# Three float32r passes with split operands for the second output projection of a two-layer hybrid decoder

## The chip, the cores and the metric

The kernel runs on one core of one Trainium2 chip, in float32. The metric is device time of one launch in microseconds (us), the median of the timed runs; less is better. TensorE (PE in the rows) multiplies, PEld is its weight load, VectorE is DVE, ScalarE is ACT, GpSimd is POOL, SyncE is SP; a q behind a name is that engine's queue.

## The reference

Two decoder layers over 512 tokens of width 1024. Each is mixer, layer norm, mixture of experts, layer norm and a gated injection. Layer 1's mixer is sparse latent attention, whose heads are joined and then mapped by one output projection:

```python
def mixer_c(x, w_in, q_norm, kv_norm, w_uq, w_uk, w_uv, w_out):
    ...
    o = lax.map(block, jnp.arange(T // Q_BLOCK))
    o = o.transpose(1, 0, 2, 3).reshape(B, T, C_HEADS * C_HEAD_DIM)
    return o @ w_out
...
def reference(...):
    for i in range(DEPTH):
        ...
        x = layer_norm(ALPHA * x + h.astype(x.dtype), ln1_g[i], ln1_b[i])
        m = hierarchical_moe(x, moe_w_group[i], moe_b_group[i], moe_w_expert[i], moe_b_expert[i],
                             moe_w_gu[i], moe_w_down[i])
        x = layer_norm(ALPHA * x + m, ln2_g[i], ln2_b[i])
        x = x + jax.nn.sigmoid(x @ ple_w_gate[i]) * (p[i] @ ple_w_proj[i])
```

`o` and `w_out` are 512x1024 and 1024x1024. `hierarchical_moe` chooses two of 32 experts for a token; an expert's weights are 1024x1024 for gate and up and 512x1024 for down, 6,144 KB together.

## The kernel before

The program is a row of blocks, each with its own instruction lists for the engines, written out by hand with semaphores; a block begins once all engines have left the one before. For layer 1 the blocks are `latents` (projections into latent space and the choice of keys), `attention`, `out_projection` (with the first layer norm, the turned copy XT of the tokens and the router's logits), `route` (which token goes to which slot of which expert) and `experts` (all 32 experts, then the second norm and the injection).

**Attention.** Tokens form four tiles of 128 (T = 4). A unit is one tile and one head; 64 units run in the order tile 3, 2, 1, 0, with 512, 384, 256 and 128 keys. All engines go through the same counter i and each works on a unit some steps behind it: TensorE scores unit i, turns unit i-6 and multiplies unit i-8 with the values; VectorE (L1893) adds the mask; ScalarE (L1919) takes the exponential; VectorE inverts the sum of unit i-2 (L1899); GpSimd (L1935) multiplies the row by it, except every fourth unit, which VectorE multiplies at step i+3 (L1904); ScalarE copies three of four turned units out of PSUM (L1838), VectorE every fourth (L1883). `finish` copies the results of half a tile's heads out of PSUM bank 6 or 7 into MC, a view of `slim[1]`: ScalarE the first half at step 0 of the next tile (L1838), VectorE the second half at step 8 (L1834), both once more behind the last unit.

**Output projection.** `out_projection` computes four tiles in two halves of 512 columns, each half in a PSUM bank over KD = 8 products (L639), `sums.full` counting the halves. VectorE adds each half to the tokens (L662), takes statistics (L190) and normalises (L198, L202); TensorE turns the tile back (L162) and computes router logits (L633) from the copy that ScalarE makes (L169). The weights w_out lie in `wide[0]`, loaded during `latents`.

**Memory and loads.** `wide[0]`, `wide[1]` (32 KB a partition) and `slim[0]`, `slim[1]` (16 KB) are two areas for experts, `pair[0]` = (`wide[1]`, `slim[0]`) and `pair[1]` = (`wide[0]`, `slim[1]`). SP issues all weight transfers in order. `load_gu` (L429) loads gate and up as two transfers of 2,048 KB, `load_dn` (L433) down as one, `load_third_gu` (L438) a third expert's gate and up into w3 and w4, `load_third_dn` (L442) its down matrix into XT. Expert 0 goes into `pair[0]` and, in `out_projection`, is loaded by `load_first` while the products run; expert 1 goes into `pair[1]` behind the last half (`then_load`, which waits for `sums.full`, 8th count, and stands behind the stores of the normalised tokens, L694, and the loads of the next norm's vectors, L211 and L212). In `experts` SP issues the next load of an area when TensorE has read the half that lay there. The rows of tokens for an expert are gathered by GpSimd (L871), turned (L883), multiplied (L898 gate and up, L912 down) and scattered (L877).

The first layer's input projection (L405) already works in float32r: ScalarE rounds an operand to float32r (L305, L314), VectorE subtracts that from the operand (L336, L343), and each float32 product becomes three of float32r: high times high, high times low, low times high.

## Time and profile before

| what | value |
|---|---|
| median of 3 runs (lowest, highest) | 1667.98 us (1664.65, 1668.8) |
| the profiled execution | 1662.05 us |
| its span, first to last instruction | 1660.2 us |
| TensorE busy | 1435.3 us, 86% |
| VectorE, ScalarE, GpSimd busy | 406.8, 305.6, 188.8 us |
| moved by DMA | 482.55 MB, mean 291 GB/s |
| layer 1: attention | 930.8 to 1013.9 us of the span |
| layer 1: output projection and first norm | 1014.3 to 1085 |
| layer 1: router, experts, injection | 1085 to the end |

Times in the rows are microseconds from the span's start. Where a row names what ended an engine's idle time, that is inferred from semaphores. An engine that is busy most of a stretch need not be what bounds it; what ends the waits says that.

### The profile page before, as it was taken

Reading aid. Unit: us, or ns where it says so; the run is one execution under the profiler, and the core shown is the slowest. Engines: PE = TensorE matmul, PEld = TensorE weight load, DVE = VectorE, ACT = ScalarE, POOL = GpSimd, SP = SyncE. Lnnn points to the kernel's source line nnn. Section 1 sums busy time; section 2 is a strip of 40 time slices with the busy share of each in tenths; the row PEclk is TensorE's granted clock in tenths of the full one; section 3 lists DMA queues with packets and bytes.
Section 4 is the critical chain, followed back from the end, with each engine's and each line's share of the span. In section 5 each row is a group of like instructions: output and inputs, shape, how many; then the busy total and the mean of one; then the engine's idle time right before and its main releaser. Section 6 shows DMA issues by size and latency. Waiting matters only on the chain. (4 is left out here: it accounts for less than half of the span.)

```text
span 1660.2 us, 16843 instructions
## 1 busy us (share of the span) xinstructions
PE 1435.3 (86%) x6032; PEld 656.7 (40%) x6032; DVE 406.8 (25%) x1016; ACT 305.6 (18%) x622; POOL 188.8 (11%) x317
## 2 busy tenths in 40 slices
PE   6998978998888789879999989959988788889887
PEld 5885443332223233224444454533322223333333
DVE  3424341000000011044068353340000000011072
ACT  3212011111011011012234563011111011101121
POOL 0000001221111111100000221011111111111100
PEclk9999978999999999999999999969999999999999
DMA  7106357999999999994200004279999999999840
GB/s 283 51 26 266 139 201 314 396 427 430 429 428 429 428 429 428 425 376 165 108 1 1 1 2 187 122 304 385 429 429 428 431 429 428 429 428 426 362 189 38
DMA packets 78305, 482.55 MB, mean 291 GB/s; under 512 B 18400, under 2 KB 20452, under 8 KB 45480
## 3 DMA queue, kind: packets, MB, share of 16 engines
q1 hardware_dynamic: 65800, 463.76, 67.2%
q0 software_dynamic: 10240, 16.82, 2.7%
q10 hardware_dynamic: 2208, 1.20, 0.2%
q8 instruction: 37, 0.61, 0.1%
q14 instruction: 20, 0.16, 0.0%
HBM read 474.91 MB, written 23.59 MB: 300 GB/s over the span
## 5 line engine op out<-in xcount | busy, mean ns | idle before, releaser
L898 PE MATMUL PS<-wide,w 128*64 128x512 f32 x1984 | 447.3, 600 | 47.6 <-ACT w L917 29.0
L912 PE MATMUL PS<-slim,w 128*64 128x512 f32 x992 | 256.2, 663 | 77.4 <-issue 76.1
L898 PEld LDWEIGHTS PS<-wide,w 128*64 128x64 f32 x1984 | 136.6, 137 | 326.5 <-issue 259.5
L912 PEld LDWEIGHTS PS<-slim,w 128*64 128x64 f32 x992 | 85.0, 150 | 242.8 <-issue 240.6
L924 DVE TENSOR_TENSOR w<-w,PS 128x256 f32<-128x256 f32 x64 | 26.9, 421 | 530.9 <-ACT w L921 530.9
L1164 PE MATMUL PS<-wide,XT 128*128 128x512 f32 x256 | 116.5, 612 | 2.3 <-ACT XT L169 2.3
L921 ACT ACTIVATE w<-PS 128x256 f32<-128x256 f32 x64 | 24.6, 384 | 498.9 <-PE PS L898 498.9
L927 DVE COPY w<-PS 128x256 f32<-128x256 f32 x64 | 27.2, 425 | 300.0 <-PE PS L905 300.0
L1477 ACT ACTIVATE w<-PS,w 128x512 f32<-128x512 f32 x62 | 42.6, 688 | 315.2 <-PE PS L912 315.2
L1344 POOL COPY w<-w 128x1 uint32 (+1 forms) x62 | 11.3, 182 | 656.7 <-ACT w L1477 656.7
L1164 PEld LDWEIGHTS PS<-wide,XT 128*128 128x128 f32 x256 | 49.3, 196 | 62.8 <-issue 59.6
L871 POOL DMA_INDIRECT w<-x_rows,w x64 | 67.2, 1050 | 55.0 <-POOL w L1337 53.7
L877 POOL DMA_INDIRECT y_rows<-w x62 | 63.6, 1027 | 54.8 <-POOL w L1344 54.8
L639 PE MATMUL PS<-wide,slim 128*128 128x512 f32 x128 | 56.0, 594 | 1.1 <-PEq L1840 1.1
L883 PE MATMUL PS<-ident,w 128*128 128x128 f32 x256 | 42.8, 291 | 8.3 <-DMA w<-x_rows,w 8.2
L169 ACT ACTIVATE XT<-PS 128x512 f32<-128x512 f32 x40 | 21.7, 594 | 149.6 <-PE PS L162 149.6
L917 ACT ACTIVATE w<-PS 128x512 f32<-128x512 f32 x64 | 38.2, 597 | 44.5 <-PE PS L883 42.8
L405 PE MATMUL PS<-x_high,w_high 128*128 128x512 f32 x96 | 38.2, 398 | 8.1 <-DVE w_low L343 8.1
L905 PEld LDWEIGHTS PS<-ident,w 128*128 128x128 f32 x128 | 20.1, 206 | 56.7 <-issue 53.0
L1935 POOL TENSOR_SCALAR w<-w 128x512 f32<-128x512 f32 (+3 forms) x48 | 26.6, 555 | 128.2 <-DVE w L1899 127.7
L883 PEld LDWEIGHTS PS<-ident,w 128*128 128x128 f32 x256 | 36.8, 211 | 9.4 <-DMA w<-x_rows,w 9.4
L1919 ACT ACTIVATE w<-w 128x512 f32<-128x512 f32 (+3 forms) x64 | 35.6, 556 | 23.9 <-DVE w L1893 23.7
(225 smaller groups left out, 1494.5 us busy)
## 6 DMA issues: line engine op xcount, KB each, us to landing
wide<-in_moe_w_gu SPq DMA_DIRECT2D x124, 2048.0 KB, 25.4
slim<-in_moe_w_down SPq DMA_DIRECT2D x62, 2048.0 KB, 25.4
w<-in_moe_w_gu SPq DMA_DIRECT2D x4, 2048.0 KB, 18.7
wide<-in_ple_w_gate SPq DMA_DIRECT2D x4, 2048.0 KB, 13.8
w<-in_ab_w_in SPq DMA_DIRECT2D x2, 2048.0 KB, 14.0
w_in<-in_ab_w_in SPq DMA_DIRECT2D x2, 2048.0 KB, 7.5
x_rows<-X SPq DMA_DIRECT2D x8, 512.0 KB, 2.8
XT<-in_moe_w_down SPq DMA_DIRECT2D x2, 2048.0 KB, 20.8
```

Of the source, the lines that this page charges most:

```text
L405: m = pe.matmul(PS[:, j % 8, :], lhsT, rhs, start=(k == 0 and r == 0), stop=(k == KD - 1 and r == 2))
L639: m = pe.matmul(PS[:, 2 * t + c, :], mixed[:, k, t * P:(t + 1) * P], w_halves[c][:, k, :], start=(k == 0), stop=(k == KD - 1))
L871: pool.indirect_dma_start(out=xg[q], out_offset=None, in_=x_half, in_offset=bass.IndirectOffsetOnAxis(ap=index, axis=0), bounds_check=2 * ...
L877: pool.indirect_dma_start(out=y_rows, out_offset=bass.IndirectOffsetOnAxis(ap=index, axis=0), in_=ys[q], in_offset=None, bounds_check=4 * ...
L883: m = pe.transpose(PS[:, q, c * P:(c + 1) * P], xg[q].rearrange("p (f c) -> p c f", c=4)[:, c, :], ident[:, :])
L898: m = pe.matmul(PS[u * SLOTS:(u + 1) * SLOTS, 2 + q, :], xeT[q][:, k, :], gu[k].rearrange("p (a u c) -> p a u c", a=2, u=2)[:, :, u, :], s ...
L912: m = pe.matmul(PS[u * SLOTS:(u + 1) * SLOTS, 6 + q, :], gT[:, k, :], dn[k][:, u * NB:(u + 1) * NB], start=(k == 0), stop=(k == FF // P - 1))
L917: return act.activation(xeT[q].rearrange("p (u c) s -> p c u s", u=2), PS[:, q, :].rearrange("p (c u s) -> p c u s", c=4, u=2), ACT.Copy)
L927: return dve.tensor_copy(gT.rearrange("p (u c) s -> p c u s", u=2), PS[:, 4 + q, 0:2 * P].rearrange("p (c u s) -> p c u s", c=2, u=2))
L1164: m = pe.matmul(PS[:, self.gate_bank(u), :], XT[:, k, t * P:(t + 1) * P], WG[:, k, c * NB:(c + 1) * NB], start=(k == 0), stop=(k == KD - 1))
L1477: act.activation(ys[q], PS[:, 6 + q, :], ACT.Copy, scale=R["gate_of"][:, bass.ds(expert(q, i), 1)]).then_inc(s_y[q], 1)
L1919: act.activation(g, g, ACT.Exp, bias=nmax[:, i:i + 1], scale=-1.0, accum_out=rsum[:, i:i + 1]).then_inc(s_p, 1)
```

## The change

1. `out_projection` takes its products from a function. For layer 0 they are as before. For layer 1 each float32 product becomes three of float32r, 192 instead of 64.
2. The operands are split during attention. `finish` becomes two steps: ScalarE copies a half bank into `mixed_high` (float32r, in `slim[1]`), then VectorE subtracts it from the bank into `mixed_low` (in the first half of `wide[1]`). ScalarE does so for both halves (steps 0 and 8), VectorE at steps 2 and 10. For the weights ScalarE copies a piece of 128x512 into `w_out_high` (second half of `wide[1]`, and `slim[0]`) at every fourth step, and GpSimd subtracts it from the raw weights into `w_out_low`, in place in `wide[0]`: 16 pieces.
3. Since `wide[1]` and `slim[0]` now hold split operands until the last product, expert 0's three transfers move from `load_first` to `then_load`, ahead of expert 1's.

```diff
-        def out_projection(l, mixed, w_halves, w_sems, load_first, then_load):
+        def out_projection(l, products, w_sems, load_first, then_load):
...
-                            for k in range(KD):
-                                m = pe.matmul(PS[:, 2 * t + c, :], mixed[:, k, t * P:(t + 1) * P],
-                                              w_halves[c][:, k, :], start=(k == 0), stop=(k == KD - 1))
+                            pairs = products(t, c)
+                            for r, (lhsT, rhs) in enumerate(pairs):
+                                m = pe.matmul(PS[:, 2 * t + c, :], lhsT, rhs, start=(r == 0),
+                                              stop=(r == len(pairs) - 1))
...
+        MCH = three(again("mixed_high", "slim1", 0, 4096)[:, :], SEQ)
+        MCL = three(again("mixed_low", "wide1", 0, 4096)[:, :], SEQ)
+        WO = three(wide[0][:, :], D)
+        WOL = three(again("w_out_low", "wide0", 0, 8192)[:, :], D)
+        WOH = [three(again("w_out_high0", "wide1", 4096, 4096)[:, :], D), three(again("w_out_high1", "slim0", 0, 4096)[:, :], D)]
...
+            def finish_high(act, half, nth):
+
+                high, low, ps = mixed_of(half, nth)
+                act.wait_ge(s_pv, AH // 2 * nth + 4 * half + 4)
+                act.activation(high, ps, ACT.Copy).then_inc(s_mh, 1)
+
+            def finish_low(dve, half, nth):
+
+                high, low, ps = mixed_of(half, nth)
+                dve.wait_ge(s_mh, 2 * nth + half + 1)
+                dve.tensor_tensor(low, ps, high, ALU.subtract).then_inc(s_o[half], 1)
...
-                        if i % AH == 8 and i >= AH:
-                            finish(dve, dve.tensor_copy, 1, i // AH - 1)
-                    finish(dve, dve.tensor_copy, 1, T - 1)
+                        if i % AH == 2 and AH <= i < N:
+                            finish_low(dve, 0, i // AH - 1)
+                        if i % AH == 10 and AH <= i < N:
+                            finish_low(dve, 1, i // AH - 1)
+                    finish_low(dve, 0, T - 1)
+                    finish_low(dve, 1, T - 1)
...
+                        if i % 4 == 2 and i < N:
+                            raw, high, low = out_pieces(i // 4)
+                            if i < 4:
+                                act.wait_ge(s_cwout, 16)
+                            act.activation(high, raw, ACT.Copy).then_inc(s_wh, 1)
+                    finish_high(act, 0, T - 1)
+                    finish_high(act, 1, T - 1)
...
+                        if i % 4 == 3:
+                            raw, high, low = out_pieces(i // 4)
+                            pool.wait_ge(s_wh, i // 4 + 1)
+                            pool.tensor_tensor(low, raw, high, ALU.subtract).then_inc(s_wl, 1)
...
         def before_out(l):
             def load_first(sp):
-                if l == 1:
-                    load_gu(sp, 1, 0, 0)
-                    load_dn(sp, 1, 0, 0)
                 load_third_gu(sp, l)
...
         def after_out(l):
             def then_load(sp, sums):
                 sums.wait_full(sp, 7)
+                if l == 1:
+                    load_gu(sp, 1, 0, 0)
+                    load_dn(sp, 1, 0, 0)
                 load_gu(sp, l, 1, 1)
                 load_dn(sp, l, 1, 1)
...
+            high = [WOH[k // 4][:, k % 4, cs] for k in range(KD)]
+            return [pair for k in range(KD) for pair in ((MCH[:, k, ts], high[k]), (MCH[:, k, ts], WOL[:, k, cs]),
+                                                         (MCL[:, k, ts], high[k]))]
```

What stands in a row on the engines is shown at two places. First, the whole of GpSimd's list in attention (buffer numbers are left out in names; w is one of w1 to w4). Before:

```order
L1928 UNCONDITIONAL_BRANCH
L1935 ISA
L1935 TENSOR_SCALAR w<-w 128x512 x12
L1935 TENSOR_SCALAR w<-w 128x384 x12
L1935 TENSOR_SCALAR w<-w 128x256 x12
L1935 TENSOR_SCALAR w<-w 128x128 x12
```

After, its beginning, in tile 3:

```order
L1973 ISA
L1973 TENSOR_SCALAR w<-w 128x512 x3
L1977 TENSOR_TENSOR w_out_low<-wide,w_out_high_1105 128x512
L1973 TENSOR_SCALAR w<-w 128x512 x3
L1977 TENSOR_TENSOR w_out_low<-wide,w_out_high_1105 128x512
```

A subtraction stands behind every third multiplication, through all tiles.

ScalarE at the change from tile 3 to tile 2. Before (L1919 the exponential, L1838 with `w<-PS` the copy of a turned unit, with `slim<-PS` the `finish` copy):

```order
L1919 ACTIVATE w<-w 128x512
L1919 ACTIVATE w<-w 128x384
L1838 ACTIVATE w<-PS 128x512
L1838 ACTIVATE slim<-PS 128x4x128
L1919 ACTIVATE w<-w 128x384
```

After:

```order
L1865 ACTIVATE w<-PS 128x512
L1962 ACTIVATE w_out_high_1105<-wide 128x512
L1949 ACTIVATE w<-w 128x512
L1949 ACTIVATE w<-w 128x384
L1865 ACTIVATE w<-PS 128x512
L1856 ACTIVATE mixed_high<-PS 128x4x128
L1949 ACTIVATE w<-w 128x384
```

A piece of the weights now stands ahead of the last exponential of a group of four units.

Second, SP's list in the output projection of layer 1, and what follows it. Before:

```order
L682 DMA w<-in_moe_b_expert 128x32
L429 DMA wide<-in_moe_w_gu 128x4096 x2
L433 DMA slim<-in_moe_w_down 128x2x2048
L438 DMA w<-in_moe_w_gu 128x4096 x2
...
L694 DMA x_rows<-X 128x1024 x4
L211 DMA ln_g<-in_ln_g 128x1024
L212 DMA ln_b<-in_ln_b 128x1024
L429 DMA wide<-in_moe_w_gu 128x4096 x2
L433 DMA slim<-in_moe_w_down 128x2x2048
L624 UNCONDITIONAL_BRANCH
```

After:

```order
L690 DMA w<-in_moe_b_expert 128x32
L445 DMA w<-in_moe_w_gu 128x4096 x2
...
L702 DMA x_rows<-X 128x1024 x4
L218 DMA ln_g<-in_ln_g 128x1024
L219 DMA ln_b<-in_ln_b 128x1024
L436 DMA wide<-in_moe_w_gu 128x4096 x2
L440 DMA slim<-in_moe_w_down 128x2x2048
L436 DMA wide<-in_moe_w_gu 128x4096 x2
L440 DMA slim<-in_moe_w_down 128x2x2048
L631 UNCONDITIONAL_BRANCH
```

Three transfers of 2,048 KB moved from the start of the block to its end, in front of three others and of the branch that ends the block.

## Rows read from the trace of the kernel before

**Rows 1.** The page: span, GB/s in 40 equal slices, expert weight loads.
```profile
span 1660.2 us, 16843 instructions
...
GB/s 283 51 26 266 139 201 314 396 427 430 429 428 429 428 429 428 425 376 165 108 1 1 1 2 187 122 304 385 429 429 428 431 429 428 429 428 426 362 189 38
...
wide<-in_moe_w_gu SPq DMA_DIRECT2D x124, 2048.0 KB, 25.4
```

**Rows 2.** The chain that ended last, within layer 1's experts: start, us, what.
```profile
1258.72 26.64 DMA wide<-in_moe_w_gu
...
1285.41 3.68 PE PS L898 x16
```

**Rows 3.** Stretches: length, busy per engine (count), clock, DMA share, GB/s.
```profile
1104.00:1120.00 16.00, 10.53 (x42) 4.03 (x42) 5.43 (x21) 2.86 (x4) 2.82 (x5) 0.76 0.51 187
1120.00:1150.00 30.00, 28.59 (x136) 10.31 (x138) 1.69 (x4) 3.34 (x6) 4.90 (x8) 1.00 0.93 372
...
1240.00:1540.00 300.00, 252.46 (x1082) 90.34 (x1079) 23.40 (x49) 32.09 (x58) 46.61 (x76) 0.95 1.01 429
```

**Rows 4.** Timeline, both projections: start, us, engine, line, operation, idle before.
```profile
1059.18 7.03 PE L639 MATMUL PS<-wide,slim 128*128 128x512 f32 x16
1066.06 1.87 PE L633 MATMUL PS<-w,XT 128*128 128x36 f32 x16
...
86.29 0.39 PE L405 MATMUL PS<-w_high,x_high 128*128 128x512 f32 x1
...
129.58 0.39 PE L405 MATMUL PS<-w_high,x_low 128*128 128x512 f32 x1
...
1074.91 0.69 DVE L662 SCALAR_TENSOR_TENSOR X<-X,PS 128x512 f32<-128x512 f32 x1 [7.24 <-PE PS L639]
...
1078.00 1.28 DVE L202 SCALAR_TENSOR_TENSOR X<-X,rstd,ln_b 128x1024 f32<-128x1024 f32 x1
```

**Rows 5.** Attention and the first split: groups, a stretch, and timeline rows.
```profile
L314 ACT ACTIVATE w_high<-w_in 128x1024 fp32r<-128x1024 f32 x4 | 4.0, 1049 | 5.2 <-DMA w_in<-in_ab_w_in 5.2
...
L336 DVE TENSOR_TENSOR x_low<-PS,x_high 128x512 fp32r<-128x512 f32 x8 | 4.9, 683 | 8.6 <-ACT x_high L305 8.6
...
996.80:1013.90 17.10, 13.86 (x119) 8.45 (x118) 9.00 (x61) 11.83 (x51) 4.95 (x13) 1.00 0.01 1
...
1000.69 0.40 ACT L1919 ACTIVATE w<-w 128x128 f32<-128x128 f32 x1 [0.45 <-DVE w L1893]
...
946.06 0.69 POOL L1935 TENSOR_SCALAR w<-w 128x512 f32<-128x512 f32 x1 [1.34 <-DVE w L1899]
950.31 0.85 POOL L1935 TENSOR_SCALAR w<-w 128x512 f32<-128x512 f32 x1 [3.56 <-DVE w L1899]
...
1000.83 0.37 POOL L1935 TENSOR_SCALAR w<-w 128x128 f32<-128x128 f32 x1 [0.69 <-DVE w L1899]
1003.12 0.84 POOL L1935 TENSOR_SCALAR w<-w 128x128 f32<-128x128 f32 x2 [1.92 <-DVE w L1899]
```

**Rows 6.** Timeline: the last two `finish` copies of attention.
```profile
1012.62 0.60 ACT L1838 ACTIVATE slim<-PS 128x512 f32<-128x512 f32 x1
...
1013.35 0.69 DVE L1834 COPY slim<-PS 128x512 f32<-128x512 f32 x1 [1.40 <-PE PS L1871]
```

**Rows 7.** Timeline of SP's queue behind the output projection.
```profile
1082.08 0.91 SPq L429 DMA_DIRECT2D wide<-in_moe_w_gu  x2
1083.03 0.96 SPq L433 DMA_DIRECT2D slim<-in_moe_w_down  x1
...
1114.10 10.03 SPq L429 DMA_DIRECT2D wide<-in_moe_w_gu  x3
```

**Rows 8.** The chain: the first gather, and one within the plateau.
```profile
1101.08 6.07 DMA w<-x_rows,w
...
1195.69 9.03 DMA w<-x_rows,w
```

More of the change, by code:

```diff
@@ L54, in build, with again @@
     with ctx:
+        home = {}
         def sb(name, shape, dt=F32):
+            home[name] = -(-nc.sbuf_base // 32) * 32
             return ctx.enter_context(nc.sbuf_tensor(name, shape, dt))
+        def again(name, of, first, n):
+            return nc.alloc_sbuf_tensor_at(name, [P, n], F32R, offset=home[of] + 4 * first)
         def lasting(name):
@@ L1810, in build, with out_pieces @@
         rden = w2[:, 2176:2240]
-        MC = three(slim[1][:, :], SEQ)
+        MCH = three(again("mixed_high", "slim1", 0, 4096)[:, :], SEQ)
[3 more added lines that the diff above has]
+        WOH = [three(again("w_out_high0", "wide1", 4096, 4096)[:, :], D), three(again("w_out_high1", "slim0", 0, 4096)[:, :], D)]
+        def out_pieces(p):
+            k, cs = p // 2, slice((p % 2) * NB, (p % 2 + 1) * NB)
+            return WO[:, k, cs], WOH[k // 4][:, k % 4, cs], WOL[:, k, cs]
         def attention():
@@ L1824, in attention, with mixed_of @@
             s_ptc = [sem(f"{n}_ptc_{e}") for e in ("act", "dve")]
-            s_o = [sem(f"{n}_o_{e}") for e in ("act", "dve")]
+            s_o = [sem(f"{n}_o_{half}") for half in range(2)]
+            s_mh, s_wh, s_wl = sem(f"{n}_mixed_high"), sem(f"{n}_w_high"), sem(f"{n}_w_low")
             def so_far(owner, j):
                 return owner[:j + 1].count(owner[j])
-            def finish(eng, copy, half, nth):
+            def mixed_of(half, nth):
                 t = ORDER[nth]
-                eng.wait_ge(s_pv, AH // 2 * nth + 4 * half + 4)
-                copy(MC[:, 4 * half:4 * half + 4, t * P:(t + 1) * P], three(PS[:, 6 + half, :], P))\
-                    .then_inc(s_o[half], 1)
+                return [m[:, 4 * half:4 * half + 4, t * P:(t + 1) * P] for m in (MCH, MCL)] + [three(PS[:, 6 + half, :], P)]
+            def finish_high(act, half, nth):
[6 more added lines that the diff above has]
+                dve.tensor_tensor(low, ps, high, ALU.subtract).then_inc(s_o[half], 1)
             def plain(act):
@@ L1923, in _ @@
                             copy_turned(act, plain(act), j)
-                        if i % AH == 0 and i >= AH and i < N:
-                            finish(act, plain(act), 0, i // AH - 1)
-                    finish(act, plain(act), 0, T - 1)
+                        if i % AH == 0 and AH <= i < N:
+                            finish_high(act, 0, i // AH - 1)
+                        if i % AH == 8 and AH <= i < N:
+                            finish_high(act, 1, i // AH - 1)
+                        if i % 4 == 2 and i < N:
[5 more added lines that the diff above has]
+                    finish_high(act, 1, T - 1)
                 @block.gpsimd
@@ L1935, in _ @@
                             pool.tensor_scalar(g, g, rden[:, i:i + 1], 1.0, ALU.mult, ALU.mult).then_inc(s_n[0], 1)
+                        if i % 4 == 3:
+                            raw, high, low = out_pieces(i // 4)
+                            pool.wait_ge(s_wh, i // 4 + 1)
+                            pool.tensor_tensor(low, raw, high, ALU.subtract).then_inc(s_wl, 1)
+                    pool.wait_ge(s_wl, N // 4)
             Stages.end()
@@ L1971, in store_tiles, with first_products, second_products @@
             sp.wait_ge(s_out, 16 * T)
-        out_projection(0, MT, w_out0, s_wout, before_out(0), after_out(0))
+        def first_products(t, c):
+            return [(MT[:, k, t * P:(t + 1) * P], w_out0[c][:, k, :]) for k in range(KD)]
+        def second_products(t, c):
+            ts, cs = slice(t * P, (t + 1) * P), slice(c * NB, (c + 1) * NB)
+            high = [WOH[k // 4][:, k % 4, cs] for k in range(KD)]
+            return [pair for k in range(KD) for pair in ((MCH[:, k, ts], high[k]), (MCH[:, k, ts], WOL[:, k, cs]),
+                                                         (MCL[:, k, ts], high[k]))]
+        out_projection(0, first_products, s_wout, before_out(0), after_out(0))
         layer_end(0, next_layer_loads, lambda sp, s_done: None, True)
@@ L1976, in build @@
         attention()
-        WO = three(wide[0][:, :], D)
-        out_projection(1, MC, [WO[:, :, 0:NB], WO[:, :, NB:D]], [s_cwout], before_out(1), after_out(1))
+        out_projection(1, second_products, [s_cwout], before_out(1), after_out(1))
         layer_end(1, lambda sp, norm: None, store_tiles, False)
```

## The prediction

> **What bounds the kernel now.** I read the page first. Its GB/s line has two plateaus near 429, one for each layer's mixture-of-experts stage [rows 1]; the second covers about 460 of the span's 1660.2 us. The chain that ended last shows what holds such a plateau: between two runs of L898, the gate/up products, lies a transfer of a weight half that takes 26.64 us from issue to landing, and L898 starts again as it lands [rows 2]. So there the weight stream, not TensorE, sets the pace. The stretches by time say when that stream is full: its DMA share is 1.01 at 429 GB/s from 1240 to 1540, but only 0.51 between 1104 and 1120 and 0.93 from there to 1150 [rows 3]. Before the plateau the engines set the pace. The output projection of layer 1 (L639) kept TensorE busy, while VectorE waited 7.24 us for its last half tile [rows 4]; the layer norm, router and gather that follow wait for it.
>
> So there are two currencies. Time saved ahead of 1082 moves the start of the weight stream earlier, us for us; bytes moved behind 1082 lengthen the stream, unless they fall into the hole at 1104.
>
> **Step 1, the products: 11.4 us less.** Sixteen recorded passes of L639 are eight float32 products, one half tile: they started at 1059.18 and the next group (L633) at 1066.06 [rows 4], so 6.88 us, 0.859 us a product, and 55.0 us for 64. The new loop issues 192 float32r products of the same shape and operand order. The first projection (L405) already has such: 192 of them from 86.29 to 129.58, hence (129.58 - 86.29) / 191 = 0.2266 us each [rows 4], and 192 cost 43.5 us. They come in the same groups of 24 for one bank, and one half tile costs 5.4 us, so a tile 10.9. VectorE's work on the second half of a tile ran from 1074.91 to 1078.00 + 1.28 [rows 4], 4.4 us, and on the first half it has two more passes of 0.69: about 6 of 10.9, so it stays ahead, and the tail behind the last product is as before. 55.0 - 43.5 = 11.5; I take 11.4 for the change of pitch at group edges. The bounds: the same 192 products at 0.2266, and nothing saved if they went at 0.286 us.
>
> The Trainium skill (FP8 and Floating Point Precision, TensorE Precision Notes) says that full float32 takes four passes through the array. Three passes would then cost three quarters, the step would save 13.7 us, and the total would be 2.3 us lower. The rows give 3 x 0.2266 / 0.859 = 0.79, and the rows decide.
>
> **Step 2, the weight split during attention: 0.3 us more.** ScalarE gets 16 copies of 128x512 and 4 more `finish` copies, GpSimd 16 subtractions, VectorE 4 more `finish` passes. All of it sits in loops that are waited for, so each needs cover.
>
> ScalarE: a copy of 128x512 took 0.60 us [rows 6], and a float32r copy of 128x1024 1.049 [rows 5]. I take 0.6 for a piece; twenty make 12 us. ScalarE is busy 11.83 of 17.10 us even in the last, tightest tile [rows 5]. A copy stands behind unit 4k+2, and the next two-unit step begins with ScalarE waiting 0.45 us for VectorE [rows 5]. So 0.6 us is mostly absorbed within two steps. Ends: 0 and 12 us; I take 0.3, near the bottom, since ScalarE is idle for 5 of those 17 us.
>
> GpSimd: the trace has no two-input operation on it. One input of 128x512 took 0.69 and one of 128x128 0.37 us [rows 5], so 0.83 ns a column over 0.26. Two inputs cost between 0.69 and, with the column price doubled, 1.11. The subtraction stands behind the third of each three multiplications. There GpSimd waits: from 946.75 to 950.31 (3.56 us) in the widest tile, 1.92 us in the narrowest [rows 5]. Either value is hidden.
>
> VectorE: the half-bank copies at step 8 go; two subtractions come at steps 2 and 10, 0.683 us each by the like operation of the first projection [rows 5]. VectorE waits in front of most steps for a score, and these steps are not those in which TensorE waits for its turned copy. Nothing.
>
> **Step 3, the end of attention: 0.7 us more.** Before, ScalarE (1012.62) and VectorE (1013.35) emptied the last two banks independently [rows 6]. Now the last bank goes through ScalarE (0.6) and then VectorE (0.68). So VectorE's operation starts one ScalarE copy and a hand-over later.
>
> **Step 4, the preload: 4.3 us more.** The SP queue issued the first two transfers behind the projection at 1082.08 and the third at 1083.03 [rows 7]: expert 1's weights. Now expert 0's three transfers of 2,048 KB go ahead of them: 6.29 MB. At 0.429 MB/us [rows 3] they are 14.7 us of stream. What do they displace? In the hole the stream lacks (1.01 - 0.51) x 16 = 8.0 us of full share, and from 1120 to 1150 (1.01 - 0.93) x 30 = 2.4 [rows 3]. Together 10.4: 14.7 - 10.4 = 4.3 us that the stream ends later against its own start. By bytes instead of share the hole is 9.0 + 4.0 = 13.0, the loss 1.7; that is the low end. The high end is 14.7, if none of the hole were filled. It is filled as long as the first refill, issued at 1114.10 after half of expert 0's products [rows 7], comes before the longer backlog ends. The 8.0 us missing ahead of that refill put the old backlog's end near 1106, so the new one ends near 1121. Expert 0's own weights are first in the queue: 6.29 MB behind 1082 are in by about 1098, and its first product comes later than the gather's landing at 1107 [rows 8].
>
> A new delay lies here: the first gather now meets a full stream. It took 6.07 us when the stream was running dry, and 9.03 in the plateau [rows 8]. So expert 0 starts up to 3 us later, and the refill comes near 1117, still before 1121. It costs nothing more.
>
> **The sum.** -11.4 + 0.3 + 0.7 + 4.3 = -6.1 us. The profiled execution took 1662.05 us (span 1660.2), which becomes 1655.9. It lies 5.9 under the median of 1667.98, on which I predict: 1661.9 us, 0.37% less. A measurement of this kernel can tell about 0.3%, 5.0 us, from no change.
>
> **Rivals.**
> A, **the stream runs dry after all.** For: SP issues three more transfers before the barrier that opens the router, and the gather waits 3 us longer. A refill after 1121 leaves a hole, us for us. With 3 us from the gather and up to 4 from SP it is just reached, and then the 2.4 us missing behind 1120 stay too: some 3 us are lost, 1664.9, no change. Against: SP needed 1.9 us for its three [rows 7].
>
> B, **the preload is free.** If TensorE rather than the stream bounded the stage, only -10.4 stays: 1657.6. For: near the plateau's end the chain runs over TensorE for long. Against: the share stays at 1.01 to 1540 [rows 3].
>
> C, **attention becomes slower than the products gain.** The mechanism is GpSimd's subtraction: multiplications of the next group queue behind it, and TensorE's turns need them. Between 3.56 and 1.92 us of cover I interpolate 3.0 and 2.5 for the middle tiles. At 3.0 us a subtraction, four groups in each of the last two tiles lose 0.5 and 1.1: 6.4 us, the whole gain. At 3.5 us: 4 x (0.5 + 1.0 + 1.6) = 12.4, and 1674.3 us. Against: it takes nearly three times the doubled price of step 2. A row that speaks for friction is the multiplication at 950.31: 0.85 us instead of 0.69, beside VectorE's division [rows 5]. The Trainium skill (SBUF — State Buffer, Who interferes with whom) says that GpSimd and VectorE's fast mode take a shared port by turns, each for a whole instruction. By that rule a subtraction that outlasts its cover would hold up VectorE's division too, which would make the rival dearer; inside the cover it changes nothing.
>
> D, **the float32r products do not keep their pitch** with operands split elsewhere and a router in between: at 0.25 us 48.0 instead of 43.5, and 1666.4, no change. Against: 192 in a row kept it [rows 4].
>
> **Chances.** Forecast 0.55; A 0.20; B 0.07; C 0.10; D 0.08. The forecast lies 1.1 us beyond the edge of what can be told, so about a quarter of it counts as no change, and a third of A as faster: faster 0.41 + 0.06 + 0.07 = 0.54, slower 0.10, the same 0.36. The range takes in step 4's low end and B below, A and D above: 1656.5 to 1668.0.
>
> **What would show it.** Step 1: 192 products at 0.227 us, the last bank full about 10.4 us earlier against the span's start. Step 2: attention still about 83 us, GpSimd's subtractions near 1.1 us, and its waits shorter by that. Step 3: a ScalarE and then a VectorE row at the end. Step 4: a DMA share near 1 from the first load on without the hole, expert 0 starting 2 to 3 us later behind the router than before, and the plateau's end about 6 us earlier. I am wrong if subtractions exceed 2 us, if the share drops below 0.9 once the stream has begun, or if the last weight half lands less than 4 us earlier.

## The result, and the profile after

| | median (runs) | profiled | span |
|---|---|---|---|
| before | 1666.76 (1662.70 to 1672.85, 6) | 1662.05 | 1660.2 |
| after | 1657.32 (1655.17 to 1659.17, 6) | 1657.87 | 1656.0 |

The ratio is 0.9949 (95%: 0.9934 to 0.9963), so 8.5 us faster by the ratio (6.2 to 11.0). The forecast was 1661.9, in a range from 1656.5: the measured median lies in the range, 0.8 us above its low end.

The page of after, span and GB/s in 40 slices, for [rows 1]:

```profile
span 1656.0 us, 17015 instructions
...
GB/s 284 51 26 267 138 217 297 387 428 429 428 429 430 428 429 428 420 384 186 108 1 0 1 1 115 74 423 404 429 428 428 430 430 428 428 430 427 372 174 38
```

Stretches of after (length, then busy us and count per engine, granted clock, DMA share, GB/s). The first is attention; the others answer [rows 3]:

```profile
932.52:1017.68 85.16, 72.55 (x608) 44.37 (x608) 50.30 (x232) 67.07 (x201) 46.28 (x64) 1.00 0.01 1
...
1080.00:1094.00 14.00, 6.27 (x40) 5.95 (x40) 8.44 (x48) 1.45 (x9) 1.10 (x4) 0.50 1.01 429
...
1104.00:1110.00 6.00, 6.00 (x20) 1.81 (x22) 0.00 (x0) 1.19 (x1) 1.07 (x1) 0.65 1.02 424
1110.00:1120.00 10.00, 8.37 (x42) 3.07 (x40) 0.84 (x2) 0.98 (x2) 0.00 (x0) 1.00 1.02 436
...
1130.00:1140.00 10.00, 9.31 (x48) 3.41 (x44) 0.84 (x2) 1.67 (x3) 1.23 (x2) 1.00 0.89 358
...
1240.00:1530.00 290.00, 243.21 (x1054) 87.77 (x1056) 22.55 (x47) 31.30 (x56) 46.59 (x76) 0.96 1.01 428
```

The hole at 1104 is gone, as predicted; one of 0.89 is left at 1130 to 1140, just under the 0.9 that the prediction had named as a sign of being wrong. Attention takes 85.2 us. Before, the same stretch (from the exponential's table load to the first load of `out_projection`) took 83.5:

```profile
930.79:1014.32 83.53, 71.75 (x600) 43.66 (x598) 48.53 (x229) 66.00 (x198) 46.18 (x64) 1.00 0.01 1
```

The timeline of the projection in after (start, us, engine, line), for [rows 4]; L647 is the product, L670 VectorE's addition, L209 the end of the norm:

```profile
1054.78 0.39 PE L647 MATMUL PS<-w_out_high,mixed_high 128*128 128x512 f32 x1
1055.01 0.40 PE L647 MATMUL PS<-w_out_low,mixed_high 128*128 128x512 f32 x1
...
1067.03 0.69 DVE L670 SCALAR_TENSOR_TENSOR X<-X,PS 128x512 f32<-128x512 f32 x1 [5.86 <-PE PS L647]
...
1070.11 1.29 DVE L209 SCALAR_TENSOR_TENSOR X<-X,rstd,ln_b 128x1024 f32<-128x1024 f32 x1
```

From the projection's start to the last full bank it is 1067.03 - 1017.68 = 49.35 us; before, with the 1074.91 of [rows 4], 1074.91 - 1014.32 = 60.59. That is 11.2 us less. SP's queue behind it in after, for [rows 7], and below it one row of before that stands in the same place as 1072.27:

```profile
1072.27 0.78 SPq L219 DMA_DIRECT2D ln_b<-in_ln_b  x1
1073.09 1.33 SPq L436 DMA_DIRECT2D wide<-in_moe_w_gu  x2
...
1109.79 13.45 SPq L436 DMA_DIRECT2D wide<-in_moe_w_gu  x4
```
```profile
1080.15 1.89 SPq L212 DMA_DIRECT2D ln_b<-in_ln_b  x1
```

Two times of these rows are used for every kernel below: S, the first expert load behind the projection (1073.09; before 1082.08), and R, the first refill (1109.79; before 1114.10). What after's first gather and expert 0's products took, by the chain and the timeline, for [rows 8]:

```profile
1093.79 8.30 DMA w<-x_rows,w
```
```profile
1103.95 9.16 PE L906 MATMUL PS<-wide,w 128*64 128x512 f32 x32 [0.69 <-ACT w L925]
...
1115.72 7.09 PE L906 MATMUL PS<-wide,w 128*64 128x512 f32 x32 [0.69 <-ACT w L925]
```

**Where the time went**, from attention's start to the span's end, by these rows: attention +1.63; projection to S, 1073.09 - 1017.68 = 55.41 against 67.76, -12.35; S to the end, 582.9 (1656.0 - 1073.09) against 578.1 (1660.2 - 1082.08), +4.8. Sum -5.9 (723.5 against 729.4), where -6.1 was forecast. On the span's own clock the last weight half landed only 4.3 us earlier (1539.96 + 24.97 against 1543.87 + 25.39, by the chains), where about 6 was forecast and less than 4 was to be a sign of being wrong. For attention itself began 1.7 us later in this profile, though nothing ahead of it was changed: TensorE's granted clock was 0.84 from 890 to 900, where in the kernel before it was 1.00. A second profile of after (`after_again`) began at 930.41 and took 723.3 from there.

### The profile page after: what moved, and what is told of

It is laid out like the page before. It is cut to its first block and busy times, and to the rows that moved or that the text cites. A ratio compares the mean times of both kernels' runs of the same rounds, so it can differ in the third digit from the quotient of the medians.

```text
span 1656.0 us, 17015 instructions
## 1 busy us (share of the span) xinstructions
PE 1425.3 (86%) x6096; PEld 669.3 (40%) x6096; DVE 409.6 (25%) x1020; ACT 314.9 (19%) x642; POOL 208.4 (13%) x333
## 5 line engine op out<-in xcount | busy, mean ns | idle before, releaser
L1352 POOL COPY w<-w 128x1 uint32 (+1 forms) x62 | 11.2, 181 | 660.8 <-ACT w L1485 660.8
L891 PE MATMUL PS<-ident,w 128*128 128x128 f32 x256 | 42.8, 291 | 11.5 <-DMA w<-x_rows,w 11.1
L1920 DVE CUSTOM_DVE_ANT_0 w<-PS,w 128x512 f32<-128x512 f32 (+2 forms) x48 | 26.3, 551 | 51.8 <-PE PS L1877 51.8
## 6 DMA issues: line engine op xcount, KB each, us to landing
wide<-in_ple_w_gate SPq DMA_DIRECT2D x4, 2048.0 KB, 13.7
w<-in_ab_w_in SPq DMA_DIRECT2D x2, 2048.0 KB, 13.6
```

The costliest lines, as they stand in the source:

```text
L891: m = pe.transpose(PS[:, q, c * P:(c + 1) * P], xg[q].rearrange("p (f c) -> p c f", c=4)[:, c, :], ident[:, :])
```

## The experiments

A table of all profiled kernels comes first, since most of the argument stands on it. `lost` is the time that the stream did not move bytes in the 80 us behind S: 80 x (1 - GB/s / 429), the GB/s from the stretch S to S+80. Three of these stretches (before, after, warm_again):

```profile
1082.08:1162.08 80.00, 61.48 (x291) 28.94 (x293) 19.00 (x89) 10.61 (x23) 13.79 (x22) 0.81 0.87 349
```
```profile
1073.09:1153.09 80.00, 58.38 (x272) 27.93 (x272) 18.61 (x89) 11.68 (x25) 12.07 (x20) 0.78 0.99 408
```
```profile
1069.42:1149.42 80.00, 69.98 (x321) 32.44 (x322) 18.63 (x89) 11.18 (x25) 13.83 (x22) 0.94 1.01 418
```

| kernel | S | R | lost | end | end-R | end-S-lost |
|---|---|---|---|---|---|---|
| before | 1082.1 | 1114.1 | 14.9 | 1660.2 | 546.1 | 563.2 + 14.7 |
| before_look | 1082.9 | 1116.5 | 18.1 | 1663.9 | 547.4 | 562.9 + 14.7 |
| preload_only | 1081.2 | 1117.2 | 3.4 | 1664.1 | 546.9 | 579.6 |
| after | 1073.1 | 1109.8 | 3.9 | 1656.0 | 546.2 | 579.0 |
| after_again | 1071.0 | 1107.6 | 3.9 | 1653.7 | 546.2 | 578.8 |
| two_passes | 1058.2 | 1094.3 | 4.5 | 1641.2 | 547.0 | 578.5 |
| early_loads | 1065.9 | 1111.8 | 12.3 | 1658.2 | 546.4 | 580.0 |
| half_early | 1064.4 | 1109.9 | 13.6 | 1659.7 | 549.8 | 581.7 |
| late_expert1 | 1072.0 | 1105.6 | 8.2 | 1661.2 | 555.6 | 581.0 |
| pool_twice | 1077.6 | 1114.6 | 6.0 | 1664.1 | 549.5 | 580.6 |
| act_twice | 1077.9 | 1114.7 | 4.1 | 1661.6 | 546.9 | 579.6 |
| warm_fill | 1075.2 | 1106.6 | 2.1 | 1656.5 | 549.9 | 579.2 |
| warm_again | 1069.4 | 1102.6 | 2.1 | 1651.4 | 548.8 | 579.9 |
| warm_early | 1062.5 | 1106.1 | 10.1 | 1652.1 | 546.0 | 579.5 |

In the two kernels with the old preload, 14.7 us of stream (expert 0) lie ahead of S and are added. So the last column is 577.6 to 581.7 in all fourteen: **the end is the stream's start, plus its bytes, plus what it loses at its beginning**, to within 4 us. That is the currency of the prediction's step 4. The balance closes no better than that, so it can't decide about an effect of 1 or 2 us. And where the stream has lost more than some 2 us, R goes with the end: end-R is 546.0 to 547.4 in nine of the eleven kernels other than warm_fill, warm_again and late_expert1. The other two, half_early and pool_twice, lie near 550. In both expert 1's first products ran for a part at half clock (8.78 instead of 7.09 us), but they did in before_look too, at 547.4; so what the 3 us are is open.

**after_again and preload_only.** The changed kernel once more, and before with expert 0's three loads moved behind the projection and nothing else:

```
-                if l == 1:
-                    load_gu(sp, 1, 0, 0)
-                    load_dn(sp, 1, 0, 0)      # in load_first, beside the products
...
+                if l == 1:
+                    load_gu(sp, 1, 0, 0)
+                    load_dn(sp, 1, 0, 0)      # in then_load, ahead of expert 1's
```

> The changed kernel once more. The first profiles read -6.1 us from the start of attention to the end (932.52 to 1656.0 against 930.79 to 1660.2), while the medians read -9.4 and the ratio -8.5 us. Theory (the sum of the four steps, -6.1): with more runs the ratio comes near 0.9963, say 0.9955 to 0.9970. Rival (there is another gain that the profile of that execution missed): it stays at 0.9949 or below, and the profile then shows more than 6.1 us between the same two points.

> The kernel before with expert 0's three loads moved behind the last half tile, nothing else. Theory (the added 6.29 MB fall mostly into the hole of the weight stream): 4.3 us slower, 1.7 to 5. Rival 1 (the stage is not bound by the stream, the preload is free): 0. Rival 2 (nothing of the hole is filled): 14.7 us slower. In the profile the DMA share between the first of these loads and the first refill should be near 1.01 where before it was 0.51, and the first gather should land 2 to 3 us later after its issue.

Measured: after_again 1656.63 (1655.87 to 1658.37, 6 runs), 0.9953 (0.9935 to 0.9971), between its two expectations and with an interval that holds both. preload_only 1666.65 (12 runs), 1.0015 (1.0 to 1.003): 0 to 5 us slower, middle 2.5. Its profile gives 733.1 us from attention's start to the end. That is 3.7 more than before's first profile (729.4), but only 0.5 more than before's second (before_look below, 732.6). By the table the stream got 14.7 us longer and lost 11.5 less than in the first, net 3.2, and 14.7 less than in the second, net 0. So what the preload costs depends on how wide the hole is in the execution that it is compared with. The forecast of 4.3 is in the runs' interval, in its upper half.

**two_passes** leaves out the product of the high piece of the activations and the low piece of the weight, one of the three that make a float32 product. It is there for the price, not for use:

```
-  return [pair for k in range(KD) for pair in ((MCH[:, k, ts], high[k]), (MCH[:, k, ts], WOL[:, k, cs]),
-                                               (MCL[:, k, ts], high[k]))]
+  return [pair for k in range(KD) for pair in ((MCH[:, k, ts], high[k]), (MCL[:, k, ts], high[k]))]
```

> The changed kernel without the product high x low: 128 instead of 192 float32r products, one of three passes left out; all splitting as before. Theory (time ahead of the weight stream goes through us for us, since both the stream's start and the router move): 64 x 0.2266 = 14.5 us faster than the changed kernel. Rival (something else is next in the projection, VectorE's norm of about 5.9 us a tile against 7.3 of products): 10 us or less.

Measured: 1643.59, ratio 0.9876 (0.9852 to 0.9899), 13.0 below after_again. The projection's last bank was full 34.87 us behind its start, 14.5 earlier than the 49.35 of after and just 64 x 0.2266. Of that 13.1 arrived at S: the issue of `ln_b` ahead of the loads took 2.12 us here, as in before (1.89), and 0.78 in after. Why it takes either is open. From S on nothing changed. So time saved in the products arrives at the end, less what the issue of one small load took back.

**early_loads, late_expert1, half_early, warm_early** move the loads against the router. early_loads issues all six loads of experts 0 and 1 once the last bank is full and the last tile's store to `x_rows` from ScalarE's queue; half_early only expert 0's two wide loads, ahead of that store on SP:

```
 for t in range(T):
+    if l == 1 and t == T - 1:
+        sums.wait_full(sp, 7)
+        load_gu(sp, 1, 0, 0)
     sp.wait_ge(norm.done, t + 1)
     sp.dma_start(x_rows...)
```

late_expert1 instead holds expert 1's three loads back to the start of `experts`. warm_early is half_early with the extra matmuls of warm_fill (below).

> The changed kernel with the six loads of experts 0 and 1 issued as soon as the last half tile is done, ahead of the last store of tokens (which goes through ScalarE's queue instead) and of the norm's vectors: the stream starts some 5 us earlier, near 1067 instead of 1072.5, the router does not. Theory (in the changed kernel the first refill, at 1109.8, meets a stream that has just about run out, so the router's path and the stream bound it together): 1 to 2 us faster than the changed kernel, and the hole ahead of the refill comes back, 3 to 5 us wide. Rival (the stream alone bounds the stage): 5 us faster.

> The changed kernel with expert 1's three loads of layer 1 issued when its experts' stage begins (about 1103) instead of right behind expert 0's: the gather of expert 0's rows then runs with fewer transfers beside it. If only the order of time at which the first refill may start mattered (it would be some 2 us earlier with a gather of 6 us), this would be 2 us faster than the changed kernel, ratio 0.994. If the stream also bounds: the 14.7 us of expert 1 stand in front of the refill, which can move its bytes from about 1118 instead of 1110; some 2 us of that come back in the stretch 1130 to 1150, where the stream has room: 5 to 7 us slower than the changed kernel, ratio 0.998 to 1.0.

> The changed kernel with expert 0's two wide loads of layer 1 issued as soon as the projection's last product is done, ahead of the last tile's store to x_rows (about 1067 instead of 1073); the other loads stay where they are. So the stream of weights starts some 5 us earlier, and the router should not start later, since it waits for the last logits until 1078. Theory (two bounds: the end comes no earlier than the first refill plus 546 us and no earlier than the stream's start plus some 581 us; in the changed kernel the first is the later one by 1.7): the refill stays, so 0 to 1 us slower or faster than the changed kernel, ratio 0.9945 to 0.9955. Rival (the stream's start alone sets the end): 5 us faster, ratio 0.992.

> Both edits together: the extra matmuls at TensorE's idle places (the refill 3.6 us earlier in warm_fill) and expert 0's two wide loads ahead of the last store (the stream 5 us earlier). Theory of two bounds: each edit alone runs into the other bound, both together move both, the refill by 3.6 us and the stream by 5: 3 to 4 us faster than the changed kernel in layer 1, 2 us faster than warm_again, ratio 0.990. Rival 1 (stream's start alone): as half_early, 5 us faster than the changed kernel even without the fillers. Rival 2 (the last store, now behind 4 MB of weights, holds the router back): no faster than warm_again.

Measured: early_loads 1660.62, 0.9975 (0.9963 to 0.9987); late_expert1 1661.18, 0.9980 (0.9969 to 0.9991); half_early 1660.15, 0.9969 (0.9959 to 0.9980); warm_early 1654.84, 0.9941 (0.9928 to 0.9954). None of the first three gains on after, and three expectations of mine fell: early_loads was to be 1 to 2 us faster and is 4 slower, half_early was to be level and is 3 slower, and warm_early was to be 2 us faster than warm_again and is 1.3 slower by the medians, as its rival 2 had it. late_expert1 came out near its second branch (5 to 7 slower), at 4 to 4.5. SP's queue in half_early shows the reason:

```profile
1064.43 0.81 SPq L436 DMA_DIRECT2D wide<-in_moe_w_gu  x2
1068.84 0.33 SPq L705 DMA_DIRECT2D x_rows<-X  x1
...
1079.36 0.38 SPq L449 DMA_DIRECT2D XT<-in_moe_w_down  x1
```

The stream starts 49.3 us behind the projection's start instead of 55.4. But the last store of tokens, 0.5 MB, now goes out behind 4 MB of weights. It landed 10.1 us after its issue, in after 2.9. The block ends only when it has landed, and the next block's first load on SP (L449) comes 149.4 us after attention's start instead of 146.0. It is not the place in SP's queue alone that does it: in early_loads the same store was issued from ScalarE's queue, took 9.8 us, and L449 came 150.8 us after attention's start. The refill follows, the stream runs dry ahead of it (13.6 us lost instead of 3.9), and the early start is given back with interest. Expert 1's products also ran for a part at half clock (8.78 instead of 7.09 us):

```profile
1103.23 9.96 PE L909 MATMUL PS<-wide,w 128*64 128x512 f32 x32 [0.69 <-ACT w L928]
...
1115.81 8.78 PE L909 MATMUL PS<-wide,w 128*64 128x512 f32 x32 [0.69 <-ACT w L928]
```

late_expert1 is the other half: R comes 33.7 us behind S instead of 36.7, since the gather meets less, and it is of no use: the stream stood still ahead of expert 1's loads (8.2 lost), and expert 1's bytes stand in front of the refill's. So neither end alone can be pulled. Whether both together would gain no run shows: warm_early was meant for it, but its early loads hold the store back too (L449 at 149.5 us, R at 178.1 behind attention's start, against 173.8 in warm_again), so its router was not early.

**warm_fill, warm_again.** In after TensorE's granted clock is 0.50 from 1072 to 1104 (its row 1104 to 1110 above: 0.65), a stretch in which it is little busy: norm, router and gather. These kernels give it something to do: float32 matmuls of the identity by 384 columns of X, into a PSUM bank that nobody reads, 19 more in each layer.

```
+        def filler(pe, n, bank):
+            for _ in range(n):
+                pe.matmul(PS[:, bank, P:NB], ident[:, :], X[:, 0, 0:NB - P], start=True, stop=True)
...
+                    filler(pe, 1, 1)     # ahead of logits(T - 2), and of logits(T - 1)
+                    filler(pe, 4, 7)     # start of route
+                    filler(pe, 3, 7)     # behind the rank sums
+                    filler(pe, 10, 6)    # behind the gates' sums in experts
```

> The changed kernel with extra float32 matmuls of the identity by 384 columns of X into a bank of PSUM that nobody reads, at TensorE's idle places of both layers: one each before the last two tiles' logits, 4 at the router's start, 3 after the rank sums, 10 after the gates' sums. The profile of the changed kernel has the granted clock at 1.2 GHz from 1071 to 1107. Theory (the end follows the first refill at a constant 546 us): the turn of the last tile (1.97 to 1.09 us), its logits (3.63 to 1.8), the slots' sum (3.67 to 1.9) and expert 0's first products (9.19 to 7.1) shorten by 6.5 us together in layer 1, the first refill comes 4 to 6.5 us earlier and the end with it; layer 0 gives 0 to 6 more: 4 to 12 us faster than the changed kernel, ratio 0.988 to 0.993. Rival 1 (the stream of weights sets the end by its own start): nothing moves, ratio 0.995. Rival 2 (the clock does not rise for these matmuls, or they get in the way of the real ones): 0 to 5 us slower than the changed kernel, and the windows of the router still show 0.50.

> warm_fill once more, for a second profile (the first fell on the slowest of its five runs, 1658.4 against 1651.2 to 1653.6, with a stretch of half clock in the projection) and to stand beside warm_early. Theory of two bounds: layer 1 gives 1.7 us at most over the changed kernel, since the stream's start bounds it from there, and layer 0 the rest; median 1651 to 1654, ratio 0.992. If layer 1 gives more than 2 us from attention's start to the end (723.4 us in both profiles of the changed kernel), the second bound is wrong.

Measured: 1651.55 (1651.24 to 1658.40, 5 runs), 0.9921 (0.9907 to 0.9935), and 1653.52 (1651.09 to 1655.98, 6 runs), 0.9933 (0.9921 to 0.9946). **This is the fastest version with all three products**: 12 to 13 us under before and 3 to 6 us under after by the medians; the intervals, each against before, touch that of after in warm_fill and overlap it in warm_again. Stretches and rows of warm_again:

```profile
1068.00:1074.00 6.00, 3.54 (x27) 2.84 (x25) 0.00 (x1) 1.17 (x3) 0.00 (x0) 0.95 0.92 265
1074.00:1084.00 10.00, 7.92 (x37) 4.60 (x38) 9.31 (x56) 2.65 (x10) 1.44 (x2) 0.86 1.01 422
1084.00:1094.00 10.00, 9.19 (x35) 6.42 (x35) 5.73 (x26) 0.00 (x0) 3.79 (x6) 0.66 1.02 433
1094.00:1104.00 10.00, 9.31 (x41) 4.25 (x41) 0.20 (x1) 1.88 (x2) 1.25 (x2) 1.00 0.99 419
```
```profile
1082.99 2.00 PE L763 MATMUL PS<-w 128*128 128x64 f32 x16 [0.47 <-DVE w L846]
...
1098.80 7.09 PE L915 MATMUL PS<-wide,w 128*64 128x512 f32 x32 [0.69 <-ACT w L934]
```

The clock stays at 2.4 GHz for most of it (0.95, 0.86, 0.66, 1.00), the slots' sum takes 2.00 instead of 3.67 us and expert 0's products 7.09 instead of 9.16. R comes 173.8 us behind attention's start, 3.5 earlier than in after. But the end comes only 0.8 earlier from there (722.6 against 723.4), in warm_fill not at all. So warm_fill's theory, that the end follows the refill at 546 us, failed in layer 1, though its total came out: the last 1.8 us of the stream's hole are closed, and then the stream's start is the bound, as the table's last column says. The rest of the gain came ahead of attention: it began at 928.81, and the layer 0 experts' stage ended (first load of `y_rows`) at 717.47 instead of 718.65 and 720.55. In the profile of warm_fill the projection itself lost 1.6 us, the clock being 0.74 from 1020 to 1025; it was the slowest of its five runs.

**pool_twice and act_twice** do GpSimd's subtraction, or ScalarE's copy, twice per piece of the weight, the second time into a spare buffer:

```
                             pool.tensor_tensor(w_out_low..., raw, high, ALU.subtract)
+                            pool.tensor_tensor(spare, raw, high, ALU.subtract)
...
+                            act.activation(spare, raw, ACT.Copy)
                             act.activation(w_out_high..., raw, ACT.Copy)
```

> The changed kernel with GpSimd's subtraction for the low piece of the weight done twice per tile, the second into a spare buffer that nobody reads. One subtraction took 1.27 us in the profile of the changed kernel, so two take 2.55. Theory (GpSimd's covers hold, as in the prediction's step 2): the gaps of GpSimd in attention shrink from 3.6 to 1.9 us towards the last tiles, so only the last one or two tiles are late: 1 to 4 us slower than the changed kernel, ratio to the kernel before 0.9955 to 0.9975. Rival (C, GpSimd is the bound, or VectorE is held up beside each subtraction): 16 times about 0.8 to 1.3 us, 12 to 20 us slower than the changed kernel, ratio 1.002 to 1.007.

> The changed kernel with ScalarE's copy for the high piece of the weight done twice per tile, the second into a spare buffer that nobody reads: 16 more copies of 0.62 us, 9.9 us of ScalarE. Theory (step 2: ScalarE waits for VectorE some 16 us during attention, and a copy falls into such a wait): 1 to 3 us slower than the changed kernel, ratio 0.9955 to 0.997. Rival (ScalarE sets attention's pace): all 9.9 us come on top, ratio 1.001.

Measured: pool_twice 1663.96, 0.9987 (0.9973 to 1.0000); act_twice 1663.03, 0.9994 (0.9982 to 1.0006): 6 and 7 us slower than the changed kernel by the ratios, between theory and rival. Attention took 88.3 and 89.3 us instead of 85.2: 3.1 and 4.1, which is the theory for GpSimd and a little above it for ScalarE. The rest is a second price that neither expectation had. Stretches of pool_twice across the end of attention:

```profile
1010.00:1020.00 10.00, 7.20 (x38) 3.73 (x39) 4.85 (x21) 5.72 (x22) 6.71 (x9) 0.57 0.01 2
1020.00:1025.00 5.00, 5.00 (x13) 3.84 (x13) 0.00 (x0) 1.13 (x2) 0.00 (x0) 0.50 0.51 63
```

TensorE's clock falls to 1.2 GHz between 1010 and 1015 in both kernels, and the projection begins in that state. From 1005 to 1010 TensorE was busy 3.48 us in pool_twice and 3.83 in act_twice, in after 4.28; that this tipped it is likely, not shown. From its start to S the projection took 57.9 and 57.3 us instead of 55.4. So 16 subtractions and copies fit where they are, with little to spare. The same trace shows how GpSimd holds up VectorE. A row of 128x128 that VectorE multiplies by the inverted sum (the division) took 0.27 us in the kernel before, and as long as the subtraction beside one:

```profile
1011.86 1.27 POOL L1984 TENSOR_TENSOR w_out_low<-wide,w_out_high 128x512 fp32r<-128x512 f32 x1
1011.92 1.30 DVE L1935 TENSOR_SCALAR w<-w 128x128 f32<-128x128 f32 x1
```

The Trainium skill (SBUF — State Buffer, Who interferes with whom) calls this an exclusive lock of a shared port pair; these two rows agree.

**before_look**, the kernel before once more:

> The kernel before once more, for a second profile: whether the first one's 83.5 us from attention's start to the projection's, its refill (end minus 546 us), and its bytes not moved in the first 90 us of the stream (16 us) are what it does each time. If so, 83.4 to 83.7, 546 to 547 and 15 to 17; span 1660 to 1666.

Measured: 1665.8, span 1663.9; attention to projection 83.55, as in the first profile. But 732.6 us from attention's start to the end, 3.2 more than there, and 18.1 us lost instead of 14.9. The first expected value came out (83.4 to 83.7), the second is just missed (end-R 547.4), the third clearly:

```profile
1109.82 9.98 PE L898 MATMUL PS<-wide,w 128*64 128x512 f32 x32 [0.69 <-ACT w L917]
...
1122.42 8.78 PE L898 MATMUL PS<-wide,w 128*64 128x512 f32 x32 [0.69 <-ACT w L917]
```

In the first profile these were 8.41 and 7.09. More of the products ran at half clock (granted 0.83 from 1114 to 1129 here), the refill came 1.9 us later behind attention's start, and the stream, dry at that time, passed it on. So the profile that the prediction rests on was a lucky one. Against this second profile the changed kernel gained 9.1 us from attention's start to the end (723.5 against 732.6): attention +1.6, projection to S -12.6, S to the end +1.9.

## Why the prediction was right, and where it was not

**Direction and mechanism hold**; the sum was -6.1 and the profiles' own difference from attention's start is -5.9. Term by term:

- **Step 1, -11.4: right.** 11.2 to the last bank, pitch 0.227 to 0.23 (the rows 1054.78 and 1055.01), and two_passes confirms the price of a product. Another 1.1 us came from the shorter issue of `ln_b`, which no step had. Rival D is refuted. The Trainium skill (FP8 and Floating Point Precision, TensorE Precision Notes) says four passes for full float32, by which three would have saved 13.7 us; the trace does not agree, with 11.2 us and three products at 0.79 of one.
- **Step 2, +0.3: too small.** From attention's start to the first `finish` behind the last unit it is 1015.36 - 932.52 = 82.8 against 81.8 with the 1012.62 of [rows 6], so +1.0. One price in it was wrong outright, GpSimd's subtraction. I put it between 0.69 and 1.11; the groups of after read

```profile
L1977 POOL TENSOR_TENSOR w_out_low<-wide,w_out_high 128x512 fp32r<-128x512 f32 x16 | 20.4, 1275 | 0.0
...
L1962 ACT ACTIVATE w_out_high<-wide 128x512 fp32r<-128x512 f32 x16 | 9.9, 617 | 0.0
```

  so 1.275 us, beyond my upper end: the second input cost more than doubling the column price allows. The Trainium skill (GPSIMD Engine Reference, 3.1 Elementwise — side-by-side cycle accounting) states about 2.6 cycles an element for a `tensor_tensor` with two inputs. At the page's 1.2 GHz that is an estimate of 1.11 us for 512 columns, and 1.37 with the fixed 0.26 us of my own fit: an upper end that would have held 1.275. I had not used it. The cover held in the wide tile, where the next multiplication comes 2.3 us after the subtraction is done:

```profile
948.82 1.28 POOL L1977 TENSOR_TENSOR w_out_low<-wide,w_out_high 128x512 fp32r<-128x512 f32 x1
952.41 0.85 POOL L1973 TENSOR_SCALAR w<-w 128x512 f32<-128x512 f32 x1 [2.32 <-DVE w L1926]
```

  In the last tile it does not wholly hide: VectorE's division beside it takes 0.85 instead of 0.27 us. But that is about half of the 1.0, and it need not all arrive. The other candidate is ScalarE, whose pieces of the weight stand ahead of exponentials that VectorE waits for. Before and after:

```profile
L1899 DVE RECIPROCAL w<-w 128x1 f32<-128x1 f32 x64 | 10.2, 159 | 0.2 <-ACT w L1919 0.2
```
```profile
L1926 DVE RECIPROCAL w<-w 128x1 f32<-128x1 f32 x64 | 10.1, 158 | 1.0 <-ACT w L1949 1.0
```

  This wait grew from 0.2 to 1.0 us, and is 3.3 us in act_twice, where attention got 4.1 us longer for 9.9 us of copies; in pool_twice it is 0.5, and attention got 3.1 us longer for 20.4 us of subtractions. So ScalarE's copies were the dearer addition for their length, and how the 1.0 divides between the two is not shown. Rival C did not come true, and pool_twice, at 2.55 us a piece, prices it: 3.1 us of attention, plus 2.5 for the clock in the projection. VectorE's row in after, beside the last subtraction:

```profile
1013.16 1.27 POOL L1977 TENSOR_TENSOR w_out_low<-wide,w_out_high 128x512 fp32r<-128x512 f32 x1
...
1013.66 0.85 DVE L1931 TENSOR_SCALAR w<-w 128x128 f32<-128x128 f32 x1
```

- **Step 3, +0.7: right.** From the first of the last two `finish` copies to the projection 1017.68 - 1015.36 = 2.3 us, against 1014.32 - 1012.62 = 1.7.
- **Step 4, +4.3: right in size for the execution that it was read from, too dear for the usual one, and with one sentence wrong.** The first profiles give +4.8 from S to the end, against before_look it is +1.9; preload_only has +3.7 and +0.5 against the two, and 0 to 5, middle 2.5, in its runs. The hole took up 11.0 us (14.9 less 3.9), where I had 10.4; in before_look it was 3.2 us wider. What was wrong is "it costs nothing more". The gather took 8.30 instead of 6.07 us and the first products 9.16 instead of 8.41, so the refill comes 36.7 us behind S (before 32.0), and the stream is left with a hole of 1.7 us (358 GB/s from 1130 to 1140). I had taken the backlog as long enough to hide it all. warm_again shows it: with R 3.5 us earlier the loss falls from 3.9 to 2.1, and 0.8 us arrive. Rival A's mechanism is thus there, at under 2 us instead of 3. Rival B's mechanism is not there: the share is 1.01 to 1530, and the end moved with the stream in all fourteen kernels. But its price, a preload that costs nothing, is at the edge of what preload_only's runs allow, and its number, 1657.6, is nearer to the measured 1657.3 than mine.
- **The step from profile to median failed**, and it makes nearly the whole difference between 1661.9 and 1657.3; only the width of the range kept the result inside. I carried over 5.9 us from before's profiled execution to its median. After's profiled execution lies 0.55 above its median (1657.87, 1657.32). The offset belonged to that execution of before, not to the program: before_look is 3.75 us slower, 0.5 of it ahead of attention and 3.2 behind, where the products of experts 0 and 1 took 1.6 and 1.7 us more at a lower clock. It lies near the median of before's runs, and against it the change gains 9.1 us, near the 8.5 of the ratio. The gain is larger there mainly because its wider hole takes up nearly all of the preload: step 4 costs 1.9 instead of 4.8. This rests on two profiles of before. Whether all of before's spread (1660 to 1673 us over the runs, after's 1655 to 1659) has this cause is open: preload_only spreads as widely (1663.7 to 1672.0), two_passes hardly (1643.1 to 1644.9), which fits a cause in the float32 projection as well.

## What to carry to other kernels

Where a stream of loads bounds a stage, its end is its start plus its bytes plus its holes: write these three for before, and price every edit in that sum, also the store or gather that an earlier load pushes back. Where two bounds lie within 2 us of each other (here the first refill and the stream's start), an edit that moves one alone got 0.8 us at most, and the edits that moved the stream's start pushed the refill back and lost. And the distance from one profiled execution to the median is a property of that execution; take a forecast from two profiles, or keep the offset in the range. The same holds for a hole that a term is to fall into: its width was 14.9 us in one profile and 18.1 in the other.

## What the runs showed of the hardware

- A gather of one expert's rows took 5.86, 6.07 and 6.34 us where the stream ran dry beside it (late_expert1, before, before_look), 7.48 and 6.73 where it had partly (early_loads, half_early), and 8.30 in a full one (after), beside 9.03 of [rows 8].
- The granted clock stayed at 1.2 GHz through the norm, the router and the gather, where TensorE was busy 6.3 of 14 us from 1080 to 1094 in after. With the gaps filled (7.9, 9.2 and 9.3 of 10 us in warm_again's rows) it was mostly at 2.4 GHz (0.86, 0.66 and 1.00), and work on the critical path that nobody had changed got up to 1.8 times faster. Matmuls whose result is thrown away were worth 3 to 6 us over the two layers.
- A two-input subtraction of 128x512 on GpSimd took 1.275 us, and VectorE's 0.27 us division beside it up to 1.30.
- A store of 0.5 MB landed 2.9 us after its issue with nothing ahead of it (after), 10.1 us behind 4 MB of weights on the same queue (half_early), and 9.8 us with the weights on SP's queue and the store on ScalarE's (early_loads).
- The issue of one and the same small load on SP (`ln_b`) took 0.78 us in eight kernels and 1.89 to 2.17 in three (before, before_look, two_passes); what decides it stayed open.
